# Seven-tile norm sums inside the last output tile, and a separate place for the next stage's first weight halves

## The reference, cut to what matters

```python
def rmsnorm(x, g):
    y = x * lax.rsqrt(jnp.mean(x * x, axis=-1, keepdims=True) + EPS)
    return y * g
def pre_norm(x, mod, j, g):
    return rmsnorm(x, g) * (1 + mod_chunk(mod, 3 * j + 1)) + mod_chunk(mod, 3 * j)
def post_residual(x, out, mod, j, g, w):
    return x + w * mod_chunk(mod, 3 * j + 2) * rmsnorm(out, g)
def swiglu(h, w_in, w_out):
    gate, up = jnp.split(h @ w_in, 2, axis=-1)
    return (jax.nn.silu(gate) * up) @ w_out
```

## Time and profile before

| | before |
|---|---|
| median of three runs | 1673.18 us |
| the profiled execution | span 1671.3 us; of its time outside the span nothing is recorded |
| TensorE busy | 1619.9 us, 97% of the span |
| VectorE busy | 834.8 us, 50% |
| ScalarE busy | 695.4 us, 42% |
| GpSimd busy | 41.9 us, 3% |
| mean granted TensorE clock | 0.985 |

### The profile page before, as it was taken

How to read it: one execution, slowest core, us unless ns; L and a number is a source line. 1 busy time by engine, 2 the same in 40 slices (tenths; PEclk the granted TensorE clock), 3 DMA queues, 4 the chain that set the end, 5 groups by cost and what they waited for, 6 DMA issues and landing times.

```text
span 1671.3 us, 27671 instructions
## 1 busy us (share of the span) xinstructions
PE 1619.9 (97%) x11325; PEld 1577.4 (94%) x11325; DVE 834.8 (50%) x1323; ACT 695.4 (42%) x1205; POOL 41.9 (3%) x46
## 2 busy tenths in 40 slices
PE   5999999999998999999999999999999999999997
PEld 4999999999887988999999999999999999999997
DVE  5544434463456988443434744433462866343333
ACT  3433333353453456333333633334363356333332
POOL 2000000001100000000000000000000000000000
PEclk8999999999998999999999999999999999999998
DMA  9733366667983126433333633346453465333310
GB/s 326 232 126 125 126 214 221 209 202 220 282 277 101 51 89 192 140 128 127 116 128 126 202 126 125 125 135 193 136 193 126 146 203 181 126 125 119 114 45 38
DMA packets 255663, 259.83 MB, mean 155 GB/s; under 512 B 6625, under 2 KB 253826, under 8 KB 255570
## 3 DMA queue, kind: packets, MB, share of 16 engines
q1 hardware_dynamic: 249664, 251.67, 46.6%
q10 hardware_dynamic: 4978, 4.41, 0.8%
q0 software_dynamic: 928, 2.44, 0.6%
HBM read 255.88 MB, written 2.62 MB: 155 GB/s over the span
## 4 chain that ended last, share of the span: by engine, by line
PE 88%; DVE 7%; issue 2%; ACT 2%; POOL 1%; DMA 1%; ACTq 0%; DVEq 0%; POOLq 0%
PE bank L405 25%; PE bank L406 25%; PE bank L407 25%; PE bank L1454 3%; PE bank L1498 1%; PE bank L426 1%; PE bank L427 1%; PE bank L428 1%; DVE X L1054 1%; DVE WL L372 1%; PE bank L1724 1%; PE bank L1505 1%; DVE HL L1020 1%; ACT WH L358 1%; DVE SUMS L1310 1%
## 5 line engine op out<-in xcount | busy, mean ns | idle before, releaser
L372 DVE TENSOR_TENSOR WL<-RAW,WH 128x1024 fp32r<-128x1024 f32 (+1 forms) x335 | 401.2, 1199 | 693.4 <-ACT WH L358 692.9
L358 ACT ACTIVATE WH<-RAW 128x1024 fp32r<-128x1024 f32 (+1 forms) x344 | 358.2, 1045 | 651.3 <-PE bank L407 638.6
L405 PE MATMUL bank<-HH,WH 128*128 128x384 f32 x1664 | 562.3, 338 | 7.3 <-DVE WL L372 3.1
L406 PE MATMUL bank<-HL,WH 128*128 128x384 f32 x1664 | 559.9, 336 | 0.0
L407 PE MATMUL bank<-HH,WL 128*128 128x384 f32 x1664 | 559.8, 336 | 0.0
L405 PEld LDWEIGHTS bank<-HH,WH 128*128 128x128 f32 x1664 | 313.4, 188 | 10.3 <-DVE WL L372 3.7
L407 PEld LDWEIGHTS bank<-HH,WL 128*128 128x128 f32 x1664 | 313.4, 188 | 0.0
L406 PEld LDWEIGHTS bank<-HL,WH 128*128 128x128 f32 x1664 | 313.3, 188 | 0.0
L405 PE MATMUL bank<-AH,WH 128*128 128x384 f32 x704 | 237.3, 337 | 0.0
L406 PE MATMUL bank<-AL,WH 128*128 128x384 f32 x704 | 236.6, 336 | 0.0
L407 PE MATMUL bank<-AH,WL 128*128 128x384 f32 x704 | 236.6, 336 | 0.0
(11 more groups left out here) (225 smaller groups left out, 1419.3 us busy)
## 6 DMA issues: line engine op xcount, KB each, us to landing
RAW<-in_ffn_w_in SPq DMA_DIRECT2D x88, 1024.0 KB, 5.1
RAW<-in_mod_w SPq DMA_DIRECT2D x72, 1024.0 KB, 6.7
RAW<-in_ffn_w_out SPq DMA_DIRECT2D x32, 1024.0 KB, 5.2
RAW<-in_ab_w_in SPq DMA_DIRECT2D x16, 1024.0 KB, 8.5
RAW<-in_ffn_w_out SPq DMA_DIRECT2D x16, 768.0 KB, 4.7
RAW<-in_cv_w_in SPq DMA_DIRECT2D x12, 1024.0 KB, 6.6
RAW<-in_ab_w_out SPq DMA_DIRECT2D x4, 1024.0 KB, 8.8
RAW<-in_cv_w_out SPq DMA_DIRECT2D x4, 1024.0 KB, 5.4
```

Of the source, the lines that this page charges most:

```text
L358: e.activation(WH[:, (2 * m + b) % 4, 0:nk, :], RAW[:, p, 0:nk, b * P:(b + 1) * P], ACT.Copy).then_inc(half_hi, 1)
L372: e.tensor_tensor(WL[:, k, 0:nk, :], RAW[:, p, 0:nk, b * P:(b + 1) * P], WH[:, k, 0:nk, :].bitcast(F32), ALU.subtract).then_inc(half_ready, 1)
L405: e.matmul(out, WH[:, k, kk, :], xh(kk), start=(first and kk == 0), stop=False)
L406: e.matmul(out, WH[:, k, kk, :], xl(kk), start=False, stop=False)
```

## The change

1. The sums of ACC, RSTD and ROOT over tiles 0 to 6 move from the turnover into the last output tile: `pe_half` calls them after kk = 2, 3 and 4 of an ffn's last half, after kk = 3, 4 and 6 of an even or odd one (`sums_early`, `within`). For s = 5 there is only the one of ACC, after kk = 2. The semaphore waits move with them.
2. Each sum's moving side is 48 columns wide (W7 96) and no longer 1 (2).
3. The halves h0 and h1 of the input stages 1 to 5 get memory of their own (LEAD, laid over MIX where it is dead). h0 and h1 wait for less, h2 and h3 go to the places that h0 and h1 had, and h4 and h5 to places freed by the last two output halves, so they no longer wait for `first_four`.
4. ScalarE makes h2 and h3 before tile 6's squares; VectorE makes both low parts before `add_terms(6)`. GpSimd's `half_low` goes.
5. `pe_four` waits for HH of a kk, does its 8 high matmuls, then waits for HL and does 4. In `out_four` the last kk is by bank, all of it behind HL; in `first_four` the last four matmuls free the four halves.
6. The modulation steps: 2 ahead of tile 7's sums, 4 between the spreads, 6 behind the second, 4 single ones in the first gaps of `first_four`.
7. The output loop of TensorE over two turns (s = 2, 5) is written out. The conv pads' memsets move behind the sixth half of the odd stage.

```diff
+        def w_high(st, h):
+            if leads(st) and h < 2:
+                return LEAD[LEAD_AT[int(st[-1])][h]]
+            return WH[:, place_of(st, h)]
+        def place_of(st, h):
+            return (2 * (stages[st]["m"] - stages[st]["apart"]) + h - 2 * leads(st)) % 4
+        def place_free(st, h):
+            at = 2 * stages[st]["m"] + h
+            if leads(st) and h < 2:
+                return at - h
+            return at - 1 if leads(st) and h < 6 else at + 1
...
-                    e.wait_ge(half_used, i * 12 + (2 * m + b + 1))
+                    e.wait_ge(half_used, i * 12 + place_free(st, 2 * jj + b))
...
             for kk in range(nk):
...
+                if within and kk in within:
+                    within[kk]()
...
             def turnover(s, OUT, n):        # ScalarE
-                nxt = ahead(act, split_act, s, "out", n)
+                if s < 5:
+                    for half in split_act(act, f"in{s + 1}", 1, 8):
+                        half()
                 out_tile(s, OUT, st, n, 0, 6)
-                nxt[0]()
                 tile_squares(s, st, n, 1, 7)
-                nxt[1]()
...
             def turnover(s, OUT, n):        # VectorE
+                if s < 5:
+                    for half in split_dve(dve, f"in{s + 1}", 1, 8):
+                        half()
                 add_terms(s, 6, OUT)
-                if s < 5:
-                    split_dve(dve, f"in{s + 1}", 1, 8)[0]()
-                dve.wait_ge(half_ready, 2 * stages[f"in{s}"]["m"] + 4)
...
+            def sums_early(s):              # TensorE
+                def squares():
+                    pe.wait_ge(sq_added, 6 * s + 6)
+                    sums(bank[0], ACC, one, lambda t: sum_at(t, 0), opens=True)
+                def squares_y():
+                    pe.wait_ge(y_added, 6 * s + 6)
+                    sums(bank[0], RSTD, one, lambda t: sum_at(t, 1))
+                def products():
+                    pe.wait_ge(xy_added, 6 * s + 6)
+                    sums(bank[1], ROOT, one, lambda t: sum_at(t, 0), opens=True)
+                steps = (2, 3, 4) if SUBLAYERS[s][0] == "ffn" else (3, 4, 6)
+                return dict(zip(steps, (squares, squares_y, products) if s < 5 else (squares,)))
```

More of the change, by code:

```diff
@@ L128, in ring_order, with leads @@
     return order
+def leads(st):
+    return st.startswith("in") and st != "in0"
 def plan():
@@ L135, in plan @@
         if st not in stages:
-            stages[st] = dict(m=split, q=mod)
+            stages[st] = dict(m=split, q=mod, apart=sum(1 for other in stages if leads(other)))
         place[st, n] = len(freed)
@@ L206, in trunk, with lead @@
             BQL, BKL = under("BQL", 4, NT), under("BKL", 4, NT)
+        LEAD_AT = {s: (1792, 2816, 3840, 4864) if s in (2, 5) else (1792, 8448, 9472, 10496) for s in range(1, 6)}
+        def lead(at):
+            with ExitStack() as over:
+                over.enter_context(nc.sbuf_tensor(f"BELOW_LEAD{at}", [P, at], F32))
+                return over.enter_context(nc.sbuf_tensor(f"LEAD{at}", [P, 8, P], F32R))
+        LEAD = {at: lead(at) for at in sorted({at for s in LEAD_AT for at in LEAD_AT[s]})}
         MIX = sb("MIX", [P, MIX_WORDS])
@@ L429, in pe_four @@
                 yield
[L430 to L436, removed]
-                    mm = e.matmul(outs[b], WL[:, kh[b], kk, :], HH[:, kk, :], start=False, stop=last)
-                mm.then_inc(half_used, 1)
@@ L558, in _ @@
             pool.dma_start(ST, state_hgrn[0, 0].rearrange("w h k v -> k (w h) v")).then_inc(state_landed, 16)
-            for s in range(2, 6):
-                half_low(f"in{s}")
         @block.scalar
@@ L1521, in first_four @@
-                for kk, _ in enumerate(steps, 1):
-                    if s == 0 and kk in (1, 3):
-                        open_piece((kk + 3) // 2)
-                    if s == 0 and kk in (2, 4):
-                        open_turn((kk + 2) // 2)
+                for n, _ in enumerate(steps):
+                    if s and n < 4:
+                        fill(s - 1, 12 + n, 13 + n)
+                    if s == 0 and n in (1, 5, 9):
+                        open_turn((n + 3) // 4)
+                    if s == 0 and n in (3, 7):
+                        open_piece((n + 5) // 4)
@@ new lines, in fill, with sum_at @@
+            def fill(s, a, b):
+                for n in (0, 2):
+                    k0, k1 = max(a, 4 * n), min(b, 4 * n + KD)
+                    if k0 < k1:
+                        mod_pair(BETWEEN[s], n, range(k0 - 4 * n, k1 - 4 * n))
+            one = lambda t: ONES[:, 0:SUM_COLS]
+            group = lambda t: min(t, 1)
+            def sum_at(t, k):
+                return slice((2 * t + k) * SUM_COLS, (2 * t + k + 1) * SUM_COLS)
+            def sums_early(s):
[10 more added lines that the diff above has]
+                return dict(zip(steps, (squares, squares_y, products) if s < 5 else (squares,)))
@@ L1832, in odd @@
                 mod_group("modI")
-                for _ in out_four(s, range(KD), lambda kk: pe.wait_ge(cat_ready, 8 + kk + 1)):
+                for _ in out_four(s, range(KD), lambda kk: pe.wait_ge(cat_hi, 8 + kk + 1),
+                                  lambda kk: pe.wait_ge(cat_ready, 8 + kk + 1)):
                     pass
```

171 lines of the change are left out of this document (82 added, 89 removed).

## The result

The changed kernel takes 1702.66 us (median of 4 executions, 1699.40 to 1706.32), the kernel before beside it 1672.82: ratio 1.0179, interval 1.016 to 1.0198. It is slower, as forecast, but by 30 us: 1682 was said, and the range ended at 1687.

What follows compares the result with a forecast made beforehand. TensorE is busy for 97% of the span, so only places where it is late or slow can move. The terms summed to +9.4 us on the median, 1682.6, shaded to 1682 us; range 1675 to 1687.

Steps and rivals of the forecast that it cites:

- Width 48: Sums at the turnovers: 48 columns cost 0, bounds 0 and 0.7 us per turnover, and should keep the clock up.
- C: Rival: the clock is lost in the first, fourth and fifth turnovers too, 1686 to 1688 us, chance 0.13.
- The stall (t1, t4): Last output tile of even and odd: TensorE stands 4.8 us for VectorE's additions; turnovers lengthen by 4.75 and 4.95 us.
- The clock in the stall: Work behind TensorE's stand, even and odd turnovers: half clock costs 2.3 us each, +4.6 for two; bounds 0 and 4.2.
- The clock in t0, t3, t4: First, fourth and fifth turnovers: the clock holds through the sums, winning 2.26, 1.00 and 2.7 us, together -6.0.
- ffn sums inside the tile: Last output tile of an ffn: sums moved there no longer cover tile 7's square, +0.95 us per turnover.
- modulation steps: Turnovers: the same 128 instructions each, all in TensorE's slack, cost 0; without the slack 0.2 us.
- h4 in t0 and t3: Turnovers ahead of even and odd: h4's split begins sooner, -1.4 and -1.3 us, together -2.7, bounds 0 and -3.2.
- L1080 in t1: Turnover from the even sublayer: dropping GpSimd's piece frees this line, -0.4 us.
- First stage and t5: First stage: a later split adds 0.65 us. Last turnover: ACC's sums no longer lie under the square, +0.7 us.

Runs made afterwards that it cites:

- e2: The changed kernel with W7 moved behind MIX, so EPSC, HH, HL and MIX lie where they lay before: 1687.04 us.
- h2: The kernel before with only the sums and W7 widened to 48 columns, W7 in its old place, order and waits untouched: 1675.48 us.
- e9: e8 with sums one column wide in place of 48: 1676.96 us.
- g2: The changed kernel with sums one column wide and W7 padded so that all addresses stay those of the changed kernel: 1688.77 us.
- e1: The kernel before with 188 unused words after W7, so EPSC, HH, HL and MIX lie 752 bytes higher: 1673.56 us.
- e7: e3 with the sums of even and odd sublayers behind the last tile, those of ffn still inside it: 1674.81 us.
- e8: e3 with all sums of the seven tiles behind the last tile, 48 wide: 1674.95 us, then 1671.36 us when repeated unchanged.
- e3: e2 with VectorE's additions of tile 6 ahead of the two low parts: 1673.93 us.
- f1: The changed kernel with 16 bytes between HL and MIX, so HH and HL stay at +752 and MIX lies at +768: 1695.00 us.
- f3: e8 with W7 back where the change has it, so EPSC, HH, HL and MIX lie 752 bytes up: 1682.47 us.
- f2: The changed kernel with W7 between HL and MIX, so HH and HL lie at -16 and MIX at +752: 1702.16 us.

## Why the prediction was wrong

**The step that failed is "Width 48".** It reads "Bounds: 0 ... and ... 0.02 per instruction, so 0.7 per turnover. I take 0." It priced what the edit makes TensorE do and left out what it makes the allocator do. The growth of W7 moves HH, HL and MIX by 752 bytes, and with that and the width of 48 the 384-column matmuls ran at 176.67 ns, which cost 12.9 us in this profile and 16.3 in another. e2 takes W7 away from there and gets 1687.04 in place of 1702.66. None of the rivals had such a term either; the farthest, C, ended at 1688. In the other direction the same width was credited by guess ("It should keep the clock up"); h2 and e9 show that it does in their orders.

**The stall (t1, t4): right in mechanism, size and place.** Forecast was a stand of 4.8 us behind two low parts; 4.66 and 5.02 were measured, and the two low parts take 2.35, against 2.3 worked out.

**The clock in the stall: right in kind, mis-sized in t1.** The half clock came both times. From the first addition seen to W,SQ it was to be 4.95 us at full clock; in t1 it is 647.90 - 638.92 = 8.98, a loss of 4.0 where 2.3 was taken. The step said the stretches "are 3.4 or 6.8 us long"; in t1 it was 10.2 and covered all of the work behind the stand. The stated bound, 4.2, was near. In t4 the stretch was 6.8, and t4 came out at +4.45 against +4.55. In e2, which has the same order, both stretches are 10.2 us and t4 takes +6.8, so t4's closeness here is in part the luck of one execution.

The Trainium skill, page "TensorE: Matmul & The Clock Gate", section "Why this matters for your kernels", warns of idle gaps between bursts. By it this term stands, and t1 and t4 agree: stands of 4.66 and 5.02 us, and 0.50 in both.

**The clock in t0, t3, t4: held in t0 and t3 as forecast, but not shown to be by the width.** g2 holds it there with narrow sums, and e1 holds it in t0 with narrow sums and the old order. The 2.26, 1.00 and 2.7 were read from one execution; in e1's, t0 loses nothing and t1 and t2 do. In the change's t4 the gain of 2.7 was booked beside a new stall that loses the clock again. h2, without a stall, shows the term by itself: 5.6 us against the same execution, forecast 6.0.

**ffn sums inside the tile: the sum right.** t2, which has no clock term, came out at +0.9 for +0.95. From tile 6's square to the first scaled tile it is 9.04 us before, 945.06 - 935.02 = 10.04 in the changed kernel and 10.00 in e7. But putting the sums behind the tile gives only 0.09 back (e8) as long as the two modulation steps stand ahead of them. "0" for the modulation steps holds in the change, where the square covers them, and not with the sums behind.

**h4 in t0 and t3: right in kind, too large.** In t0, from first scaled tile to h4 it is 359.77 - 337.96 = 21.81, before 22.78: -0.97, where -1.4 was said. In t3 it is 1261.70 - 1240.47 = 21.23, before 22.30: -1.07 for -1.3. TensorE now comes to h4 with the split already done and waits for nobody there, so its own work set the end.

**L1080 in t1: right.** Its successor, L1109, takes 0.16 us in t1. First stage and t5 came out within 0.25.

Without the slow pace, as e2 shows, the kernel is at 1687.04, the upper end of the range. Its profiled execution has a span 11.7 us over that of before, where 9.4 was forecast: t1 took +7.95 and t4 +6.8, both with a half-clock stretch of 10.2 us. That it is no farther off is luck: the first stage took +1.8, with a half-clock stretch of 3.4 us at 57.4 that before has not, and the even sublayer between t0 and t1 gave -3.05, with one half-clock stretch missing (404.7 in the profile of before) and one of 3.4 us in place of 6.8 (near 512). No term stood for either.

## What to carry to other kernels

When a tensor in the middle of the allocation grows, everything behind it moves: leave new or grown buffers for the end, or test the move by itself, before its cost is put down to the instructions. Compare traces matmul by matmul; a slope in a stretch without waits is a slower pace, and no view of waits shows it. Ahead of a wait that TensorE meets inside a dense stretch, see first what the engine that releases it has queued: two 1.2 us pieces in the wrong order in each of two turnovers cost 11 us between the profiles of e2 and e3, more than half of it through the clock. And before a term is read from a half-clock stretch, look at a second execution: e1 has it in another turnover.

## What the hardware showed beyond that

- The same stream of 384-column matmuls ran at 173.33, 174.67 or 176.67 ns start to start on average, at full granted clock and without idle time, for stretches of 20 to 260 us. The two longer paces were seen with HH at +752 with 48-wide sums (the changed kernel, f1, f3, h2) and with MIX at +752, HH at -16 (f2). Not seen at 0, +48, +112 and +768 with wide sums, nor at +752 with narrow ones (e1, g2). The stretches change from one execution to the next, and in three profiles (both of the changed kernel, and h2) they begin before the first wide sum has run. Why is open: neither the remainder by 64 nor that by 128 bytes nor W7's position explains all of these.
- With sums behind the tile, widening 18 one-column matmuls to 48 columns cost 0.08 us in t2 (e9 against e8_again) and kept the clock in t0 and t3.
- The same kernel (e8) falls into two groups 10 us apart by where the clock falls. A difference of 0.5% between single executions says nothing here.
